# Seven block products for the up projection in every second pair, separate PSUM banks for gate and up groups, and token sums and x updates ahead of the weights

## The reference, cut to what matters

```
def half_ffn(x, g, w_gate, w_up, w_down):
    h = rmsnorm(x, g)
    return 0.5 * ((jax.nn.silu(h @ w_gate) * (h @ w_up)) @ w_down)

xp = xp + half_ffn(xp, ln_ffn[layer, 0], ffn_w_gate[layer, 0], ffn_w_up[layer, 0], ffn_w_down[layer, 0])
```

## Time and profile before

| | us |
|---|---|
| median of 3 runs | 2202.05 |
| lowest and highest run | 2201.98, 2203.17 |
| profiled execution | 2202.66 |
| its span, first to last instruction | 2201.0 |
| mean granted TensorE clock | 0.984 |

### The profile page before, as it was taken

How to read it: one execution, slowest core, us unless ns; L and a number is a source line. 1 busy time by engine, 2 the same in 40 slices (tenths; PEclk the granted TensorE clock), 3 DMA queues, 4 the chain that set the end, 5 groups by cost and what they waited for, 6 DMA issues and landing times.

```text
span 2201.0 us, 42242 instructions
## 1 busy us (share of the span) xinstructions
PE 2130.2 (97%) x17908; PEld 2069.0 (94%) x17908; DVE 1355.8 (62%) x2124; ACT 865.4 (39%) x1232; POOL 67.3 (3%) x140
## 2 busy tenths in 40 slices
PE   7999999999988999999999999999999999999998
PEld 7999999998877899999999999999997599999997
DVE  6763775686456557636756754775657646745754
ACT  5331333344244543313424332333357735322333
POOL 0000000100100000000000000000102300000000
PEclk9999999999988999999999999999999999999999
DMA  4232232533200333322323232332324423232321
GB/s 150 87 106 87 82 106 65 135 83 81 78 7 3 91 104 90 105 86 79 108 75 106 78 106 87 112 91 77 101 68 130 151 77 106 78 111 82 116 74 62
DMA packets 318363, 199.16 MB, mean 90 GB/s; under 512 B 10007, under 2 KB 313267, under 8 KB 318169
## 3 DMA queue, kind: packets, MB, share of 16 engines
q1 hardware_dynamic: 309840, 174.49, 27.0%
q0 software_dynamic: 6160, 19.84, 3.1%
q10 hardware_dynamic: 2176, 2.15, 0.3%
HBM read 188.52 MB, written 8.05 MB: 89 GB/s over the span
## 4 chain that ended last, share of the span: by engine, by line
PE 88%; DVE 7%; ACT 2%; issue 1%; DMA 1%; ACTq 0%; DVEq 0%; SPq 0%
PE PS L2499 62%; PE PS L2520 17%; PE PS L2657 4%; DVE wlo L1604 1%; PE PS L3199 1%; PE PS L3118 1%; PE PS L3132 0%; PE PS L3101 0%; DMA stage<-in_w_in_e 0%; DVE X L2046 0%; PE PS L2510 0%; ACT whi L960 0%; PE PS L3121 0%; PE PS L3184 0%; DVE xT L1810 0%
## 5 line engine op out<-in xcount | busy, mean ns | idle before, releaser
L2499 PE MATMUL PS<-hb_h,whi 128*128 128x260 f32 x2448 | 499.5, 285 | 9.3 <-DVE hb_l L1640 6.2
L2499 PE MATMUL PS<-hb_h,wlo 128*128 128x260 f32 x2448 | 495.5, 284 | 0.0
L2499 PE MATMUL PS<-hb_l,whi 128*128 128x260 f32 x2448 | 493.8, 283 | 0.0
L2499 PEld LDWEIGHTS PS<-hb_h,whi 128*128 128x128 f32 x2448 | 381.1, 189 | 13.0 <-DVE hb_l L1640 6.8
L2499 PEld LDWEIGHTS PS<-hb_h,wlo 128*128 128x128 f32 x2448 | 378.2, 189 | 0.0
L2499 PEld LDWEIGHTS PS<-hb_l,whi 128*128 128x128 f32 x2448 | 377.8, 189 | 0.0
L1604 DVE TENSOR_TENSOR wlo<-stage,whi 128x1024 fp32r<-128x1024 f32 (+1 forms) x193 | 232.3, 1203 | 118.7 <-ACT whi L960 115.2
L960 ACT ACTIVATE whi<-stage 128x1024 fp32r<-128x1024 f32 (+1 forms) x193 | 200.0, 1038 | 126.8 <-PE PS L2520 62.7
L1604 DVE TENSOR_TENSOR wlo<-stage_x,whi 128x1024 fp32r<-128x1024 f32 (+1 forms) x148 | 175.4, 1187 | 84.6 <-ACT whi L960 83.8
L2499 PE MATMUL PS<-act_l,whi 128*128 128x260 f32 x896 | 180.8, 283 | 0.0
L1807 DVE SCALAR_TENSOR_TENSOR tmp<-PS,rstd 128x520 f32<-128x520 f32 x64 | 44.6, 697 | 220.9 <-PE PS L2499 220.9
(11 more groups left out here) (472 smaller groups left out, 3828.0 us busy)
## 6 DMA issues: line engine op xcount, KB each, us to landing
stage<-in_ffn_w_up SPq DMA_DIRECT2D x88, 512.0 KB, 3.8
stage_x<-in_ffn_w_gate SPq DMA_DIRECT2D x36, 1024.0 KB, 5.1
stage<-in_w_in_e SPq DMA_DIRECT2D x28, 512.0 KB, 3.8
stage_x<-in_ffn_w_down SPq DMA_DIRECT2D x20, 512.0 KB, 4.2
stage<-in_ffn_w_down SPq DMA_DIRECT2D x40, 256.0 KB, 2.7
stage<-in_w_in_o SPq DMA_DIRECT2D x20, 512.0 KB, 3.8
stage<-in_ffn_w_gate SPq DMA_DIRECT2D x16, 512.0 KB, 3.8
stage_x<-in_ffn_w_down SPq DMA_DIRECT2D x20, 384.0 KB, 3.7
```

The costliest lines, as they stand in the source:

```text
L2499: mm = pe.matmul(psum[:, half, :], w, x(k, half), start=first and w is hi and x is rhs_hi, stop=last and w is lo)
```

## The change

- `MODES`: pairs 2, 4, 6, 8 and 10 become "SS": their up projection is a group of seven products too. Pairs 3, 5, 7 and 9 stay "SP".
- Banks: gate groups always use banks 0 to 3, up groups banks 4 to 7 (`bank_of`). P1 of a group waits for all sums of the group before it in the same banks (`groups_place_free`); P3 now waits for P1's copy, P7 for U2, P4 for C11. `DOWN_PAIRS` and the waits that hang on it follow.
- Token sums ahead: in `head` at an up unit DVE makes ht_l before it waits for the unit, not behind the product.
- Weights and results: in a group, ACT's and DVE's work on results held over from an earlier event moves behind batch "a" of the next group (P2); silu of the odd gate tile is held over, silu or high of the even tile moves from P3 to P7, and `low` of the even up tile from P3 to P4.
- At the end of a piece's second half the update of x (and hb_l and the sum of squares) comes first, then the weights that this piece makes room for (`ahead(done)` behind, no `ahead(done - 1)` before). ACT's `square` makes hb_h ahead of the square.

```
-MODES = ("PP", "PP") + ("SP",) * 9
+MODES = ("PP", "PP") + ("SS", "SP") * 4 + ("SS",)
-DOWN_PAIRS = (2, 3, 1, 0, 2, 1, 0, 3)
+DOWN_PAIRS = (1, 0, 2, 3, 1, 0, 2, 3)
...
+        def bank_of(which, up):
+
+            return 4 * up + {"P1": 0, "P6": 1, "P2": 2, "P5": 3, "P3": 0, "P7": 1, "P4": 2}[which]
...
             def square(k, m, slot):
 
                 act.wait_ge(x_ready, KD * k + m + 1)
-                if not isinstance(m, int) or m >= 2 or k:
+                if k < LAST_NORM:
+                    act.activation(of_h(hb_h, m), two(xT[:, m, :]), ACT.Copy, scale=h_scale(k, m)).then_inc(h_hi, 1)
+                if m >= 2 or k:
                     act.wait_ge(ssum_added, KD * k + m - 1)
-                act.activation(tmp[:, slot, :], tile(xT, m), ACT.Square).then_inc(sq_ready, 1)
...
                     elif which == "P2":
                         ahead(done, own)
+                        if late:
+                            half_of(*late.pop())
...
                     elif which == "P3":
                         ahead(done, own + 2)
-                        half_of(2 * t, up)
                     elif which == "P7":
                         ahead(done, own + 3)
-                    elif which == "P4" and up:
-                        late.append(2 * t + 1)
+                        half_of(2 * t, up)
                     elif which == "P4":
-                        silu(2 * t + 1)
+                        late.append((2 * t + 1, up))
...
                 def head(n, up, done):
 
                     ahead(done - 1)
+                    if up:
+                        dve.wait_ge(t_act, X_TURNED + 2 * (KP * f + n) + 2)
+                        dve.tensor_tensor(ht_l[:, :, n, :], snapT[:], ht_h[:, :, n, :].bitcast(F32), ALU.subtract)\
+                           .then_inc(t_dve, 1)
                     reach(done)
...
                         add(q, C11_SUM, c11, p1, bank["P2"])
                         ahead(done, own)
+                        if late:
+                            low(late.pop())
...
                         if late:
                             low(late.pop())
-                        ahead(done - 1)
-                        if p:
+                        if p == 0:
+                            ahead(done - 1)
+                        else:
                             update_down(s, f, c, m, done)
                             if c:
                                 add_square(s + 1, m, m % 2)
+                            ahead(done)
...
+                def groups_place_free(t, up):
+
+                    c = t >= CHUNKS[1][0]
+                    older = [u for u in range(CHUNKS[c][0], t) if u >= HEAD]
+                    if older and MODES[older[-1]][up] == "S":
+                        g = next(e[1] for e in EVENTS if e[0] == "prod" and e[3:] == (older[-1], up))
+                        pe.wait_ge(block_sum, BLOCK_SUMS * (GROUPS * f + g + 1))
+                    elif older:
+                        pe.wait_ge(prod_ready, base + 2 * older[-1] + 2)
+                    elif c:
+                        pe.wait_ge(x_part, part + 2 * (8 if up else 6))
+                    else:
+                        pe.wait_ge(prod_ready, base + 2 * HEAD - (0 if up else 1))
+                        pe.wait_ge(gate_read, base + 2 * HEAD - (0 if up else 1))
...
-                    if which == "P7":
+                    if which == "P3":
                         pe.wait_ge(p1_copied, q + 1)
-                    elif which in newer:
-                        pe.wait_ge(block_sum, BLOCK_SUMS * q + newer[which])
-                    elif q:
-                        pe.wait_ge(block_sum, BLOCK_SUMS * (q - 1) + older[which])
+                    elif which == "P7":
+                        pe.wait_ge(block_sum, BLOCK_SUMS * q + U2_SUM)
+                    elif which == "P4":
+                        pe.wait_ge(block_sum, BLOCK_SUMS * q + C11_SUM)
```

More of the change, by code:

```diff
@@ L1059, in ffn @@
                     elif event[0] == "unit":
-                        high(event[1])
+                        if late:
+                            half_of(*late.pop())
                         if event[1] % 2 == 0:
+                            high(event[1])
                             ahead(done, at + 10)
+                        else:
+                            late.append((event[1], 1))
                     elif event[0] == "prod":
@@ L1068, in ffn @@
                         if late:
-                            high(late.pop())
-                        ahead(done - 1)
-                        if c and p:
+                            half_of(*late.pop())
+                        if p == 0:
+                            ahead(done - 1)
+                        elif c:
                             square(s + 1, m, m % 2)
+                            ahead(done)
+                        else:
+                            ahead(done)
             chain = [0]
@@ L1735, in group_step @@
                     own = BY_FIRST[f, g, "a"].n + (6 if MODES[t][1] == "P" else 4)
-                    bank = {w: PS[:, n, 0:HALF] for w, n in banks_of(q).items()}
+                    bank = {w: PS[:, bank_of(w, up), 0:HALF] for w in PRODUCTS}
                     u2, u3, p1 = (snapT[:, n, :] for n in range(3))
@@ L1773, in group_step @@
                         if up:
+                            low(2 * t)
                             late.append(2 * t + 1)
@@ L2542, in up_place_free @@
                 def up_place_free(n, c):
-                    older = [t for t in range(CHUNKS[c][0], n // 2) if MODES[t][1] == "P"]
-                    if older and older[-1] < HEAD:
+                    older = [t for t in range(CHUNKS[c][0], n // 2)]
+                    if older and older[-1] >= HEAD and MODES[older[-1]][1] == "S":
+                        g = next(e[1] for e in EVENTS if e[0] == "prod" and e[3:] == (older[-1], 1))
+                        pe.wait_ge(block_sum, BLOCK_SUMS * (GROUPS * f + g + 1))
+                    elif older and older[-1] < HEAD:
                         pe.wait_ge(prod_ready if n % 2 else gate_read, base + 2 * HEAD)
@@ L2558, in group_product @@
                         pe.wait_ge(t_dve, 5 * KP * (f + 1))
[L2559 to L2564, removed]
-                    if which == "P7":
+                    if which == "P1":
+                        groups_place_free(t, up)
+                    if which == "P3":
                         pe.wait_ge(p1_copied, q + 1)
-                    elif which in newer:
-                        pe.wait_ge(block_sum, BLOCK_SUMS * q + newer[which])
-                    elif q:
-                        pe.wait_ge(block_sum, BLOCK_SUMS * (q - 1) + older[which])
+                    elif which == "P7":
+                        pe.wait_ge(block_sum, BLOCK_SUMS * q + U2_SUM)
+                    elif which == "P4":
+                        pe.wait_ge(block_sum, BLOCK_SUMS * q + C11_SUM)
                     pe.wait_ge(lo_ready, batch.n + 1)
-                    bank = banks_of(q)[which]
+                    bank = bank_of(which, up)
                     buf = {"P1": (0, 0), "P2": (0, 1), "P3": (0, 2), "P4": (1, 3), "P5": (1, 0), "P6": (1, 1), "P7": (1, 2)}
```

36 lines of the change are left out of this document (13 added, 23 removed).

## The result

The changed kernel takes 2217.5 us (median of 4 runs, 2216.7 to 2218.7), the kernel before 2202.6 us measured beside it: a ratio of 1.0065, interval 1.0053 to 1.0077. It is 14.9 us slower; the forecast was 6.6 us faster, 2195.5 us as the median. The profiled execution took 2216.7 us, with a span of 2215.1 us against 2201.0.

What follows compares the result with a forecast made beforehand. PE, busy 97% of the span, was taken as the bound, with DVE too slow for one SS pair. From 2202.7 us profiled, -28.8 + 38.8 - 7.4 - 9.2 = -6.6 gave 2196.1, median 2195.5; range 2174 to 2217.

Steps and rivals of the forecast that it cites:

- 1 products: Five of nine pairs in each of four FFNs turn 96 matmuls into 84: 240 fewer on PE's path, -28.8 us.
- Part 2: In SS pairs DVE makes weight batch C late, so PE stalls at P6: 9.7 us per FFN, +38.8 us.
- part 4: At each head's end, ht_l ahead of the unit's wait restarts PE earlier and avoids low clock: -7.4 us.
- part 5: At FFN stage ends, x updates ahead of weights remove PE's 6.2 and 1.4 us waits and low clock: -9.2 us.
- part 3: Own banks for gate and up groups cost no instruction and change no wait of PE: 0 us.
- the walk: Operation-by-operation timing of DVE and PE from profile rows, giving stall places in SS pairs and waits at head and stage ends.
- Rival 1: Stalls at P6 of the up group in pairs 4, 8, 10 lower the clock twelve times: +21.5, 2217 us; chance 0.17.
- Rival 2: DVE keeps up if batch A is split during P1: stalls vanish, 2157 us, or halve, 2176; chance 0.13.
- Rival 3: At stage ends DVE still waits for next-stage loads, update 6 stays late, waits and low clock remain: 2205 us; chance 0.10.

Runs made afterwards that it cites:

- e2: The changed kernel with plain up units again (no SS pair), banks, new order and head kept: 2199.6 us, ratio 0.9990 to the kernel before.
- e1: The changed kernel with ht_l back behind the product in every step of the head: 2207.1 us, ratio 1.0022 to the kernel before.
- e5: The kernel before with only the x updates moved ahead of the weights at a piece's end: 2192.1 us, ratio 0.9952 to the kernel before.
- e7: The changed kernel with ht_l ahead of the unit's wait only in a head's last step: 2202.6 us, ratio 0.9997 to the kernel before.
- e3: The changed kernel with batch A of the next group allowed at P1 instead of P2, on ACT and DVE: 2184.0 us, ratio 0.9919.

## Why the prediction was wrong

Its sum against what the kernels show, in us. Parts 1 and 2 together are checked by the change less e2 (17.9), part 4 is the change less e1, part 5 is e5:

| part | forecast | measured | from |
|---|---|---|---|
| 1 products | -28.8 | -28.8 | 240 matmuls fewer |
| 2 stalls at P6 | +38.8 | +46.8 | 38.2 waited + 32 x 0.27 |
| 3 banks | 0 | not apart from 0 | e2 against e5 |
| 4 ht_l ahead | -7.4 | +10.4 | e1 |
| 5 x updates first | -9.2 | -10.9 | e5, without hb_h ahead of the square |
| sum | -6.6 | +17.5 | the change: +14.9 |

The 2.6 us between the last two figures are no more than the intervals of e1 and e5 leave open (about 2 and 4 us to either side). Two things work towards closing the gap: only 8.8 of part 4's 10.4 us are seen in the traces behind the heads, and e5 still has 0.9 us of waits that the change has not. For part 3: e2 differs from e5 by the banks, the late low parts, hb_h ahead of the square and the head; 2199.6 - 10.4 = 2189.2 against 2192.1, within the same bounds. No wait for a block sum appears after, so 0 stands as far as it can be told; no run has the banks alone.

**Part 4 is the step that failed.** It looked at the last step of each head, where the walk was right (0.75 us of waiting forecast, 0.8 to 1.0 measured in e7, the clock at 1.00 as forecast), and did not look at the steps ahead of it, which get the same new order. There the instruction that was moved had been the cover for ACT's act_h. The trace of before would have told it: the low part L1670 follows ht_l without a pause, and L1008 on ACT makes act_h between 814.91 and 815.55, in the shadow of ht_l. I costed the moved instruction's own 1.16 us and never asked what it had stood in front of. FFN 2 shows the other side: there DVE has slack in the head before (it waits for PE for 0.84, 1.68 and 0.53 us), which takes up most of what the steps grow by; the wait is 1.94 us as before, where e7 has 0.81. The clock loss that I meant to win back (twice 1.79) grew instead: the clock falls behind the fourth head too, and further behind the second. Its size was too large as well. Two such groups, one partly at the low clock and one at 1.00, took 11.87 and 10.34 us, so the clock costs 1.53; the other 0.26 is the restart behind any wait.

**Part 2 was right in mechanism, places and times, and its term was too small by 8.0 us.** The walk said 32 waits, 1.0 to 1.6 us, 9.7 per FFN at P6 and nowhere else; it was 32, 0.96 to 1.58, 9.55 per FFN, at P6 alone, with the places in the order of the walk. What it lacked is the 0.27 us that a stall costs beyond the wait that the profile lists. A hint was there: the first group behind the fourth head took 10.34 us at a clock of 1.00, where a group takes 10.08. I had read the 0.26 us only as a part of the clock's loss.

**Parts 1 and 5 held, and nothing speaks against part 3.** In part 5 the last two updates now stand ahead of the next stage's third and fourth batch. DVE at the end of the second FFN (before: the earlier trace rows):

```profile
1177.17 0.76 DVE L1644 SCALAR_TENSOR_TENSOR hb_l<-xT,prm,hb_h 128x520 fp32r<-128x520 f32 x1 [0.80 <-ACT hb_h L976]
1177.84 0.69 DVE L1651 TENSOR_TENSOR ssum<-ssum,tmp 128x520 f32<-128x520 f32 x1
1178.64 1.22 DVE L1608 TENSOR_TENSOR wlo<-stage,whi 128x1024 fp32r<-128x1024 f32 x1
1179.79 0.69 DVE L1813 SCALAR_TENSOR_TENSOR tmp<-PS,rstd 128x520 f32<-128x520 f32 x1
...
1182.01 0.76 DVE L1644 SCALAR_TENSOR_TENSOR hb_l<-xT,prm,hb_h 128x520 fp32r<-128x520 f32 x1 [0.80 <-ACT hb_h L976]
...
1183.49 1.22 DVE L1608 TENSOR_TENSOR wlo<-stage,whi 128x1024 fp32r<-128x1024 f32 x1
```

Update 6 (its hb_l at 1177.17) is through before the batch at 1178.64, update 7 (1179.79) before the one at 1183.49. 2.98 us pass from the take of tile 7 to the end of its hb_l, against the 3.0 of the walk.

**Rival 1 had the time and not the mechanism.** It wanted twelve stalls to lower the clock; none of 32 did, and e2 leaves no room for it. That its 2217 us is the measured time is chance: the same +21.5 us over the forecast came from the restarts (8.0 us) and from the head with its clock (17.8 by e1), less what part 5 brought beyond its term and what stays within the intervals. **Rival 2** was refuted for the change and right as a repair: e3 is its clause on `own - 1`, with 2184 us where it gave 2157 for all the stalls gone and 2176 for half of them. **Rival 3** is refuted by e5.

**A rule weighed.** The gaps of 1.0 to 1.6 us left the clock at 1.00 in every case, and around those of 1.9 to 7.1 us behind the heads it was lower in all four FFNs of the kernel after (gaps of 1.9 us ended either way: in e1 the one in the third FFN is followed by a low clock, the one in the fourth by 1.00). The Trainium skill (TensorE: Matmul & The Clock Gate, Part 1) has the clock follow how busy the engine has lately been; the trace agrees, in that PE is at work for 97% of the stretches between the heads (304.46 of 314 us, 295.46 of 305), where the clock is 1.00.

## What to carry to other kernels

Before an instruction is moved, ask what it stood in front of: in an in-order queue it may be the cover for another engine's answer, and every iteration that has the new order pays, not just the one that the move is for. A stall of a dense matmul stream costs more than its row, 0.27 us here, and the shortest have no row at all (a start 0.23 us late in e3); many short ones are read from the starts of the matmuls. When DVE becomes the bound of a stretch, look for where it still idles: putting the first batch of weights in that one place gave 33.5 us, and with ht_l moved only where nothing needs its cover the change becomes 36 us faster than before instead of 15 slower.

## What the runs showed of the hardware beyond the forecast

- A stream of matmuls of 260 columns that start 0.12 us apart loses 0.27 us per wait beyond the listed wait: 0.16 for the last matmul's length that is counted as busy, 0.11 behind the first one. The 32 stalls, told from e2, cost 17.9 + 28.8 = 46.7 us, and by the starts of the matmuls 46.8, where 38.2 are listed.
- 32 gaps of 1.0 to 1.6 us, 11 us apart at the closest, left the granted clock at 1.00. Gaps of 0.8 to 1.0 us behind the last three heads (e7) did too, where 1.94 and 4.26 us in the kernel after gave a mean of 0.80 to 0.89 in the stretch around them.
- At the low clock (0.5, 1.2 GHz) the same matmuls start 0.22 us apart (853.36, 853.58, 853.79 in the kernel after), against 0.12 at 1.00. The low clock in the first group behind a head cost 1.53 us (11.87 against 10.34 us).
